# A two-layer hybrid decoder step on one Trainium2 core: gate and up products of the feed-forward by seven half products, gated rows kept in DRAM between two phases

## The chip, the core and the metric

One core of one Trainium2 (trn2) chip runs the whole step as one program. The metric is the device time in microseconds; the kernel before was timed in three runs. Everything is fp32 in and out.

## What is computed

Two layers (state-space heads with latent attention, then sliding-window attention), each followed by a gated feed-forward with a causal depthwise convolution on its gate branch. 1024 prompt tokens and 8 sample tokens share all weights; `D_MODEL` is 1024 and `D_FF` is 2816. The part that the change touches, per layer:

```python
h = rmsnorm(x, norm_ffn[layer])
def conv_ffn(h, buf, w_gate, w_up, conv_w, conv_b, w_down):
    t = h.shape[1]
    g = h @ w_gate
    u = h @ w_up
    gp = jnp.concatenate([buf.astype(g.dtype), g], axis=1)
    c = conv_b
    for j in range(CONV_W):
        c = c + conv_w[j] * gp[:, j:j + t]
    out = (jax.nn.gelu(c) * u) @ w_down
    return out, gp[:, -(CONV_W - 1):]
x = x + f
```

## The kernel before

Activations are held transposed: a feature tile of 128 partitions by all 1032 tokens (`NT`). There are 8 model tiles (`KD`) and 22 ff tiles (`KF`). Every fp32 operand of a product is split into a hi part (rounded to the format fp32r) and a lo part (what is left), and a product is three matmuls per tile and 344 columns (`TT`): weight hi by x hi (L137), weight lo by x hi (L138), weight hi by x lo (L139), in `Slabs.products`. The weights come through two slots ("slabs", `s` 0 and 1): SP loads one (`load`), GpSimd (the `pool` queue) writes its hi and lo (`split`, L121 and L123), TensorE multiplies it with all 1032 columns into the PSUM tile of the slot, and an engine reads that tile out and frees it.

The feed-forward goes in four groups of ff tiles (6, 6, 5, 5). For each ff tile: gate into slot 0, up into slot 1 (8 x 3 x 3 matmuls each). VectorE multiplies gate by `rstd` (the norm's scale per token, L1515), does the convolution from `g` to `c` (two small copies L1517 and L1518 for the state, a `tensor_scalar` L1519, and for either further tap an op of 8 and one of 1024 columns, L1520 to L1526), multiplies up by `rstd` (L1530), takes ACT's gelu times `u` (L1533), and after ACT's hi copy writes the lo part (L1536). All of a group's gated rows stay in SBUF; after the group, TensorE does its down products for the 8 model tiles, and VectorE adds each to x (L1547, L1551).

Ahead of it, the out-projection runs 3 passes (layer 0) or 2 (layer 1) of 8 products; in the last pass VectorE adds each tile to x (L1609) and then, by `norm_dve`, writes the lo part (L220) and adds the squares that ACT has made (L226). `norm_act` is ACT's part of this (hi, L212, and square, L215). The sum over the features is three matmuls (`norm_sums`), the root ACT's (`norm_roots`, L237), and the inverse three reciprocals of 344 columns on VectorE (`norm_inverse`, L244), which lie beside the first gate product. The first product waits tile by tile for the lo parts (`paced`).

Each engine has its own queue in program order; they wait for each other with semaphores, and nothing reorders them. `ch.link` is a wait of VectorE for its own earlier op.

## Time and profile before

| | |
|---|---|
| median of 3 runs | 3202.59 us (3201.11 to 3202.88) |
| span of the profiled execution | 3200.6 us |
| TensorE busy | 2998.8 us (94%), 23117 matmuls |
| VectorE busy | 1803.8 us (56%) |
| GpSimd busy | 872.4 us (27%) |
| ACT busy | 602.1 us (19%) |
| DRAM read, written | 189.87 MB, 6.25 MB |

The page gives one execution; its span runs from the first to the last instruction. "Busy" is a sum over instructions, so it says what an engine did and not what it was waited for. In rows of instructions "PE" is TensorE's matmul, "PEld" its weight load, "DVE" VectorE, "POOL" GpSimd. The order of an engine's queue is not in the profile; it is shown with the change.

### The profile page before, as it was taken

What the parts mean: (1) busy time and instruction counts of PE and PEld (TensorE: products, weight loads), DVE (VectorE), ACT (ScalarE), POOL (GpSimd) and SP (SyncE); (2) the same over time, 40 slices, a digit from 0 to 9 for tenths busy, and PEclk for the clock granted to TensorE, in tenths of its full rate; (3) what the DMA queues carried; (4) which work ended last, traced back from release to release, by engine and by line L of the source; (5) the groups of instructions that cost most, each with busy time, mean ns of one, the idle gap of its engine ahead of it and who ended that gap; (6) DMA issues with size and microseconds to landing.
All of it is one profiled execution on the core that took longest, in us unless ns stands there. A gap on an engine that the chain in (4) does not pass through costs nothing. (4 is left out here: it accounts for less than half of the span.)

```text
span 3200.6 us, 58571 instructions
## 1 busy us (share of the span) xinstructions
PE 2998.8 (94%) x23117; PEld 2623.7 (82%) x23117; DVE 1803.8 (56%) x2750; ACT 602.1 (19%) x1200; POOL 872.4 (27%) x496
## 2 busy tenths in 40 slices
PE   6967999998999899999999999998889999999997
PEld 6944666665555499999999999994589999999997
DVE  8895655565888645533515345667737515335254
ACT  3111544552000112100000001106512100000001
POOL 3200000100000045444344344420044344444442
PEclk8978999998999999999999999999989999999999
DMA  2100000004777521111111111202111111111112
GB/s 101 54 14 31 15 14 14 0 26 138 225 226 227 150 95 57 46 41 51 48 51 44 42 53 39 67 23 88 53 47 56 48 51 46 41 51 36 56 39 76
DMA packets 129157, 206.34 MB, mean 64 GB/s; under 512 B 14833, under 2 KB 95729, under 8 KB 128274
## 3 DMA queue, kind: packets, MB, share of 16 engines
q1 hardware_dynamic: 90994, 162.31, 16.2%
q10 hardware_dynamic: 38016, 41.99, 4.4%
q8 instruction: 102, 1.67, 0.2%
q14 instruction: 45, 0.37, 0.0%
HBM read 189.87 MB, written 6.25 MB: 61 GB/s over the span
## 5 line engine op out<-in xcount | busy, mean ns | idle before, releaser
L121 POOL TENSOR_TENSOR sb_slab_hi<-sb_slab_raw,sb_ones 128x1024 fp32r<-128x1024 f32 (+3 forms) x214 | 344.4, 1609 | 1719.0 <-PE ps_trunk_out L139 1053.1
L137 PE MATMUL ps_trunk_out<-sb_h_hi,sb_slab_hi 128*128 128x344 f32 x2400 | 768.0, 320 | 0.0
L138 PE MATMUL ps_trunk_out<-sb_h_hi,sb_slab_lo 128*128 128x344 f32 x2400 | 764.8, 319 | 0.0
L139 PE MATMUL ps_trunk_out<-sb_h_lo,sb_slab_hi 128*128 128x344 f32 x2400 | 764.4, 319 | 0.0
L123 POOL TENSOR_TENSOR sb_slab_lo<-sb_slab_raw,sb_slab_hi 128x1024 fp32r<-128x1024 f32 (+3 forms) x214 | 488.7, 2284 | 16.7
L138 PEld LDWEIGHTS ps_trunk_out<-sb_h_hi,sb_slab_lo 128*128 128x128 f32 x2400 | 450.4, 188 | 0.6
L137 PEld LDWEIGHTS ps_trunk_out<-sb_h_hi,sb_slab_hi 128*128 128x128 f32 x2400 | 450.3, 188 | 0.6
L139 PEld LDWEIGHTS ps_trunk_out<-sb_h_lo,sb_slab_hi 128*128 128x128 f32 x2400 | 450.4, 188 | 0.0
L137 PE MATMUL ps_trunk_out<-sb_ffn_a_hi,sb_slab_hi 128*128 128x344 f32 x1026 | 327.3, 319 | 5.0 <-DVEq L1538 5.0
L139 PE MATMUL ps_trunk_out<-sb_ffn_a_lo,sb_slab_hi 128*128 128x344 f32 x1026 | 328.3, 320 | 0.0
L138 PE MATMUL ps_trunk_out<-sb_ffn_a_hi,sb_slab_lo 128*128 128x344 f32 x1026 | 326.6, 318 | 0.0
L1246 PE MATMUL ps_dec_bank<-sb_dec_ckT,sb_dec_qc 32*32 32x256 f32 x4608 | 258.1, 377 | 8.2 <-DVE sb_dec_qc L1347 7.9
L1246 PEld LDWEIGHTS ps_dec_bank<-sb_dec_ckT,sb_dec_qc 32*32 32x32 f32 x4608 | 142.0, 106 | 118.9 <-issue 13.4
L1491 ACT ACTIVATE sb_ffn_a<-sb_ffn_c 128x1032 f32<-128x1032 f32 x44 | 47.0, 1068 | 997.3 <-DVEq L1528 997.3
L1547 DVE TENSOR_TENSOR sb_z<-sb_z,ps_trunk_out 128x1032 f32 x48 | 59.0, 1230 | 300.6 <-PE ps_trunk_out L139 300.6
L137 PEld LDWEIGHTS ps_trunk_out<-sb_ffn_a_hi,sb_slab_hi 128*128 128x128 f32 x1026 | 192.8, 188 | 6.1 <-DVEq L1538 6.1
L139 PEld LDWEIGHTS ps_trunk_out<-sb_ffn_a_lo,sb_slab_hi 128*128 128x128 f32 x1026 | 192.8, 188 | 0.0
L138 PEld LDWEIGHTS ps_trunk_out<-sb_ffn_a_hi,sb_slab_lo 128*128 128x128 f32 x1026 | 192.8, 188 | 0.0
L937 POOL TENSOR_TENSOR sb_mla_diag<-sb_ident,sb_mla_rinv 128x256 f32<-128x256 f32 x64 | 39.2, 613 | 558.9 <-DVE sb_mla_rinv L1117 558.9
L1330 DVE STREAM_TRANSPOSE sb_dec_ckT<-sb_dec_ck 128x1152 f32<-128x1152 f32 x128 | 172.8, 1361 | 26.5 <-DMA sb_dec_ck<-cache 25.7
L1515 DVE TENSOR_TENSOR sb_ffn_g<-ps_trunk_out,sb_rstd 128x1032 f32<-128x1032 f32 x44 | 54.2, 1233 | 232.3 <-PE ps_trunk_out L139 232.3
L988 PE MATMUL ps_mla_bank<-sb_mla_k,sb_mla_q 96*128 96x512 f32 (+3 forms) x384 | 150.1, 502 | 1.8 <-ACT sb_mla_v L1048 1.8
(412 smaller groups left out, 4559.6 us busy)
## 6 DMA issues: line engine op xcount, KB each, us to landing
sb_slab_raw<-f_w_gu SPq DMA_DIRECT2D x88, 512.0 KB, 3.5
sb_dec_ck<-cache SPq DMA_DIRECT2D x256, 144.0 KB, 3.1
sb_dec_ck<-cache ACTq DMA_DIRECT2D x256, 144.0 KB, 2.8
sb_slab_raw<-f_w_down SPq DMA_DIRECT2D x32, 384.0 KB, 3.1
sb_slab_raw<-f_w_down SPq DMA_DIRECT2D x32, 320.0 KB, 2.8
sb_slab_raw<-e_w_out SPq DMA_DIRECT2D x24, 256.0 KB, 2.6
sb_slab_raw<-o_w_in SPq DMA_DIRECT2D x12, 512.0 KB, 3.5
sb_slab_raw<-e_w_in SPq DMA_DIRECT2D x10, 512.0 KB, 3.5
```

The source lines that it names most:

```text
L121: nc.gpsimd.tensor_tensor(hi, raw, one, ALU.mult).then_inc(self.hi_done[s], 1)
L123: nc.gpsimd.tensor_tensor(self.lo[:, s, 0:kc, :], raw, hi.bitcast(F32), ALU.subtract).then_inc(self.split_done[s], 1)
L137: nc.tensor.matmul(out[:, t, 0:TT], a, x_hi(k)[:, cols], start=k == 0, stop=False)
L138: nc.tensor.matmul(out[:, t, 0:TT], b, x_hi(k)[:, cols], start=False, stop=False)
L139: last = nc.tensor.matmul(out[:, t, 0:TT], a, x_lo(k)[:, cols], start=False, stop=k == kc - 1)
L937: nc.gpsimd.tensor_tensor(diag[:, big], ident[:, :].unsqueeze(1).broadcast_to((P, 2, P)), rinv[:, 2 * big:2 * big + 2].unsqueeze(2).broadc ...
L988: m = MM(score(u)[:, c0:c1], qg[:, h, qb * P:(qb + 1) * P], kg[:, h, c0:c1], start=True, stop=True)
L1246: m = MM(bank[quads[b], x, half * 256:half * 256 + 256], qc[quads[b], (w // NU) % 2, j, :], ckT[quads[b], x, pages, 32 * j:32 * j + 32], s ...
L1330: m = V.transpose(ckT[:, w % 2, g * GP:(g + 1) * GP, :].rearrange("p a c -> p (a c)"), ck[:, w % CKS, g * GP:(g + 1) * GP, :].rearrange("p ...
L1491: nc.scalar.activation(a[:, :], c[:, :], ACT.Gelu_apprx_tanh).then_inc(ffn_act_done, 1)
L1515: ch.link(V.tensor_tensor(v3(g[:, 2:]), slabs.out[:, 0, :, 0:TT], v3(rstd), ALU.mult))
L1547: V.tensor_tensor(xm, xm, slabs.out[:, s, :, 0:TT], ALU.add).then_inc(slabs.free[s], 1)
```

## The change

Of a ff tile, gate and up together are a product of two blocks of weights by two halves of the 8 model tiles. With the tokens cut in two halves of 516 (`HT`), this is a 2x2 by 2x2 block product, and it is done by Strassen's scheme in Winograd's form: seven products q0 to q6 of half the depth (4 model tiles) and half the tokens, in place of eight. The names in it:

- **Inputs** (`X_OF`): the blocks B11, B21, B22 of x and the sums T1 to T4, made once per layer when the out-projection ends (`x_act` with the hi parts, `x_dve` and `x_dve_last` with the sums and lo parts, `ffn_enter_act` and `ffn_enter_dve` around them). The norm's `norm_dve` now only adds squares.
- **Weights**: VectorE makes four sums per pair of gate and up (`w_sum`, 128x512 each), ACT seven hi parts (`w_high`), GpSimd seven lo parts (128x512, L1620), in place of GpSimd's two hi and two lo of 128x1024.
- **Products**: each q is 4 tiles x 2 x 3 matmuls of 258 columns (`QT`), so 168 per pair in place of 144 of 344 columns. They go into four PSUM bank pairs: bA takes q0, q3 and q5, bC q1 and q6, bB q2, bD q4.
- **Combining**: ACT copies q0 out (`s1`); VectorE makes g and u by seven more ops of 516 columns. The first conv tap moves from VectorE to ACT.
- **`ffn_left`** counts what VectorE has taken out of the banks, 7 per pair. q0 of the next pair waits for 6, q1 for 7 (which is L1832, behind the convolution).
- **Gated rows**: `c` times `u`, not scaled for the up branch, goes to DRAM by SP (`keep`). In the second phase, groups of (4, 6, 6, 6), ACT's queue loads a group back (`a_load`), VectorE scales it by `rstd` (`a_scale`, L1727), ACT writes the hi part, VectorE the lo part (`a_low`, L1732), and TensorE does the down products as before, with waits for each tile's lo part in the first product of a group.
- **First pair**: TensorE does the norm's sums behind q4; the three reciprocals stand on VectorE between the second and third of its ops. SBUF places of other tensors move with it (`m_parts` takes the out-projection's parts in the other order).

Sums, split and loads:

```diff
+def w_sum(dve, at_pair, q):
+    n = at_pair.n
+    if q == 0:
+        dve.wait_ge(slabs.raw_in[1], n(16, 16 * W_BEFORE[at_pair.layer] + 16))
+        V.tensor_tensor(wt[:, :, :], w_up[0], w_up[1], ALU.add).then_inc(ffn_sum, 1)
+    elif q == 1:
+        dve.wait_ge(slabs.raw_in[0], n(16, 16 * W_BEFORE[at_pair.layer] + 16))
+        dve.wait_ge(ffn_sum, n(4, 1))
+        V.tensor_tensor(wt2[:, :, :], wt[:, :, :], w_gate[0], ALU.subtract).then_inc(ffn_sum, 1)
+    elif q == 2:
+        dve.wait_ge(ffn_lo, n(7, 2))
+        dve.wait_ge(ffn_sum, n(4, 2))
+        V.tensor_tensor(wt[:, :, :], wt2[:, :, :], w_gate[1], ALU.subtract).then_inc(ffn_sum, 1)
+    else:
+        V.tensor_tensor(w_up[0], w_gate[0], w_up[0], ALU.subtract).then_inc(ffn_sum, 1)
...
+    def keep(p):
+        sp.wait_ge(ffn_a, p.n(1, 1))
+        sp.dma_start(a_dram[layer, one(p.f())].rearrange("a p t -> p (a t)"), c[:, :]).then_inc(ffn_out, 16)
...
+    with sp.Fori(0, KF - 1) as ci:
+        p = Pair(layer, 0, ci)
+        for s in range(2):
+            sp.wait_ge(ffn_lo, p.n(7, 6 + s))
+            sp.dma_start(slabs.raw[:, s, :, :], rows(ci + 1, s)).then_inc(slabs.raw_in[s], 16)
+        keep(p)
+    for s in range(2):
+        sp.wait_ge(ffn_lo, Pair(layer, KF - 1).n(7, 6 + s))
+        slabs.load(sp, s, n, GROUPS[0], A["f_w_down"][layer, s, :, 0:GROUPS[0], :])
+    keep(Pair(layer, KF - 1))
...
+def ffn_pool(pool, layer, n):
+    slabs.rows += KF
+    with pool.Fori(0, KF) as ci:
+        p = Pair(layer, 0, ci)
+        for q in range(7):
+            pool.wait_ge(ffn_hi, p.n(7, q + 1))
+            nc.gpsimd.tensor_tensor(w_slot(slabs.lo, q), W_FROM[q], w_slot(slabs.hi, q).bitcast(F32),
+                                    ALU.subtract).then_inc(ffn_lo, 1)
+    end = Pair(layer, KF - 1)
+    pool.wait_ge(ffn_mm, end.n(7, 5))
+    slabs.split(pool, 0, n, GROUPS[0])
+    pool.wait_ge(ffn_mm, end.n(7, 7))
+    slabs.split(pool, 1, n, GROUPS[0])
```

Entry, VectorE's part:

```diff
+        low(T1, m, T1f(m), 2 * m + 2, g_m)
+        return
+    k = m - HK
+    f0, h0 = HK + 3 * k, 2 * HK + 6 * k + 1
+    t2, t3, t4 = T2f(k), T3f(k), T4f(k)
+    dve.wait_ge(x_hi_done, n_h + h0)
+    V.scalar_tensor_tensor(out=t3, in0=second, scalar=g_m, in1=t3, op0=ALU.mult, op1=ALU.subtract).then_inc(x_f32, 1)
+    low(B21, k, first, h0 + 1, g_m)
+    dve.wait_ge(x_f32, f_at(f0 + 1))
+    V.scalar_tensor_tensor(out=t2, in0=x[:, k, HALF[0]], scalar=gain(k), in1=t3, op0=ALU.mult, op1=ALU.add).then_inc(x_f32, 1)
+    dve.wait_ge(x_f32, f_at(f0 + 2))
+    V.scalar_tensor_tensor(out=t4, in0=first, scalar=g_m, in1=t2, op0=ALU.mult, op1=ALU.subtract).then_inc(x_f32, 1)
+    low(T2, k, t2, h0 + 2)
+    low(B22, k, second, h0 + 3, g_m)
+    low(T3, k, t3, h0 + 4)
```

TensorE:

```diff
+def ffn_pe(pe, layer, n, i, last_pair=None):
+    bA, bB, bC, bD = ffn_banks()
+    bank_of = (bA, bC, bB, bA, bD, bA, bC)
+    def product(p, q, paced=False):
+        pe.wait_ge(ffn_lo, p.n(7, q + 1))
+        whi, wlo = w_slot(slabs.hi, q), w_slot(slabs.lo, q)
+        for k in range(HK):
+            if paced:
+                pe.wait_ge(x_lo_done, x_lo_count(layer, q, k))
+            for h in range(2):
+                cols = slice(h * QT, (h + 1) * QT)
+                out, xh, xl = bank_of[q][:, h], X_OF[q](k, 0)[:, cols], X_OF[q](k, 1)[:, cols]
+                nc.tensor.matmul(out, whi[:, k, :], xh, start=k == 0, stop=False)
+                nc.tensor.matmul(out, wlo[:, k, :], xh, start=False, stop=False)
+                m = nc.tensor.matmul(out, whi[:, k, :], xl, start=False, stop=k == HK - 1)
+        m.then_inc(ffn_mm, 1)
+    def products(p, first=False):
+        for q in range(7):
+            if first and q in (0, 2):
+                pe.wait_ge(slabs.free[q // 2], n + 1)
+            if q == 0 and not first:
+                pe.wait_ge(ffn_left, p.n(7, -1))
+            if q == 1 and not first:
+                pe.wait_ge(ffn_left, p.n(7, 0))
+            if q == 3:
+                pe.wait_ge(ffn_copied, p.n(1, 1))
+            if q in (5, 6):
+                pe.wait_ge(ffn_left, p.n(7, q - 4))
+                if first:
+                    pe.wait_ge(norm_root, 3 * i + q - 4)
+            product(p, q, first)
+            if first and q == 4:
+                pe.wait_ge(ffn_left, p.n(7, 2))
+                ffn_sums(pe, i)
+    products(Pair(layer, 0), True)
+    with pe.Fori(0, KF - 1) as ci:
+        products(Pair(layer, 1, ci))
+    end = Pair(layer, KF - 1)
+    pe.wait_ge(ffn_left, end.n(7, 6))
     k0 = layer * KF
     for grp, gs in enumerate(GROUPS):
-        skip = 0
-        if grp == 0:
-            slabs.products(pe, 0, n, KD, hi, lo, gate_hooks)
-            slabs.products(pe, 1, n, KD, hi, lo, up_hooks)
-            skip = 1
-        with pe.Fori(0, gs - skip) as ci:
+        g_hi, g_lo = g_parts[grp]
+        mul_hi, mul_lo = lambda k: g_hi[:, k, :], lambda k: g_lo[:, k, :]
+        by_thirds = last_pair is not None and grp + 1 == len(GROUPS)
+        slabs.products(pe, 0, n, gs, mul_hi, mul_lo,
+                       {k: (lambda k=k: pe.wait_ge(ffn_alo, k0 + FIRST[grp] + k + 1)) for k in range(gs)})
+        slabs.products(pe, 1, n, gs, mul_hi, mul_lo)
+        with pe.Fori(0, KD // 2 - 1 - by_thirds) as mi:
...
-            last_pair(pe, n + gs + KD // 2 - 1, gs)
-        n += gs + KD // 2
```

Phase 2's pieces, ACT's pair and VectorE's pair:

```diff
+def a_scale(dve, layer, grp, k):
+    uses = (4, 4, 4, 4, 3, 3)[k]
+    dve.wait_ge(chunk_in[k], 32 + 16 * (layer * uses + grp + (1 if k < 4 else 0)))
+    part = g_f32[grp][:, k, :]
+    V.tensor_tensor(part, part, rstd[:, :], ALU.mult).then_inc(ffn_scaled, 1)
...
+        act.wait_ge(ffn_mm, p.n(7, 1))
+        nc.scalar.copy(two(s1), bA).then_inc(ffn_copied, 1)
+        w_high(act, p, 4)
+        w_high(act, p, 5)
+        if last:
+            a_load(act, layer, 0, range(GROUPS[0]))
+        w_high(act, p, 6)
+        if kind == "first":
+            ffn_roots(act, i)
+        if not last:
+            w_high(act, nxt, 0)
+        act.wait_ge(ffn_left, p.n(7, 4))
+        if kind != "first" or layer:
+            act.wait_ge(ffn_out, p.n(16, 0))
+        nc.scalar.activation(c[:, :], g[:, 2:], ACT.Identity, scale=tap(2), bias=tap(3)).then_inc(ffn_tapped, 1)
+        if last:
+            a_high(act, layer, 0, (0, 1))
+        else:
+            for q in (1, 2, 3):
+                w_high(act, nxt, q)
+        act.wait_ge(ffn_conv, p.n(1, 1))
+        nc.scalar.activation(c[:, :], c[:, :], ACT.Gelu_apprx_tanh).then_inc(ffn_tapped, 1)
...
+        dve.wait_ge(ffn_mm, p.n(7, 3))
+        dve.wait_ge(ffn_copied, p.n(1, 1))
+        ch.mark(V.tensor_tensor(bB, bB, two(s1), ALU.add))
+        dve.wait_ge(ffn_mm, p.n(7, 4))
+        ch.settle()
+        V.tensor_tensor(two(s1), bA, two(s1), ALU.add).then_inc(ffn_left, 1)
+        dve.wait_ge(ffn_left, p.n(7, 1))
+        V.tensor_tensor(two(u_half[1]), two(s1), bC, ALU.subtract).then_inc(ffn_left, 1)
+        if kind == "first":
+            norm_inverse(dve, ch, i)
+        V.tensor_tensor(two(g_half[0]), bB, two(r_half[0]), ALU.mult).then_inc(ffn_left, 1)
+        if end:
+            a_scale(dve, layer, 0, 0)
+            a_scale(dve, layer, 0, 1)
+        dve.wait_ge(ffn_mm, p.n(7, 5))
+        dve.wait_ge(ffn_left, p.n(7, 2))
+        ch.link(V.tensor_tensor(bD, two(u_half[1]), bD, ALU.subtract))
+        V.tensor_tensor(two(g_half[1]), bD, two(r_half[1]), ALU.mult).then_inc(ffn_left, 1)
+        if not end:
+            w_sum(dve, nxt, 0)
+            w_sum(dve, nxt, 1)
+        dve.wait_ge(ffn_mm, p.n(7, 6))
+        V.tensor_tensor(two(u_half[1]), bA, two(u_half[1]), ALU.add).then_inc(ffn_left, 1)
+        V.tensor_tensor(two(u_half[0]), bA, two(s1), ALU.add).then_inc(ffn_left, 1)
+        if end:
+            a_low(dve, layer, 0, 0)
+            a_low(dve, layer, 0, 1)
+        dve.wait_ge(ffn_left, p.n(7, 4))
+        V.tensor_copy(tail[:, one(f), :], g[:, T:T + 2])
+        V.tensor_copy(new[:, one(f), 1, :], g[:, 2 + T:2 + NT])
+        dve.wait_ge(ffn_tapped, p.n(2, 1))
+        ch.mark(V.scalar_tensor_tensor(out=c[:, T:NT], in0=old(1), scalar=tap(1), in1=c[:, T:NT],
+                                       op0=ALU.mult, op1=ALU.add))
+        ch.link(V.scalar_tensor_tensor(out=c[:, 0:T], in0=g[:, 1:1 + T], scalar=tap(1), in1=c[:, 0:T],
+                                       op0=ALU.mult, op1=ALU.add))
+        ch.mark(V.scalar_tensor_tensor(out=c[:, T:NT], in0=old(0), scalar=tap(0), in1=c[:, T:NT],
+                                       op0=ALU.mult, op1=ALU.add))
+        V.scalar_tensor_tensor(out=c[:, 0:T], in0=g[:, 0:T], scalar=tap(0), in1=c[:, 0:T],
+                               op0=ALU.mult, op1=ALU.add).then_inc(ffn_conv, 1)
+        dve.wait_ge(ffn_mm, p.n(7, 7))
+        dve.wait_ge(ffn_left, p.n(7, 6))
+        V.tensor_tensor(two(u_half[0]), bC, two(u_half[0]), ALU.add).then_inc(ffn_left, 1)
+        if end:
+            for k in (2, 3):
+                a_scale(dve, layer, 0, k)
+            for k in (2, 3):
+                a_low(dve, layer, 0, k)
+        else:
+            w_sum(dve, nxt, 2)
+            w_sum(dve, nxt, 3)
+        dve.wait_ge(ffn_tapped, p.n(2, 2))
+        dve.wait_ge(ffn_left, p.n(7, 7))
+        V.tensor_tensor(c[:, :], c[:, :], u[:, :], ALU.mult).then_inc(ffn_a, 1)
```

How the order moves. VectorE's queue for one ff tile in the loop of the kernel before (register and semaphore rows left out):

```order
L1515 TENSOR_TENSOR sb_ffn_g<-ps_trunk_out,sb_rstd 128x1032 [waits slab_mm_done0]
L1517 COPY sb_ffn_tail<-sb_ffn_g 128x2
L1518 COPY sb_ffn_new<-sb_ffn_g 128x8
L1519 TENSOR_SCALAR sb_ffn_c<-sb_ffn_g,sb_ffn_taps 128x1032
L1520 SCALAR_TENSOR_TENSOR sb_ffn_c<-sb_ffn_past,sb_ffn_taps,sb_ffn_c 128x8
L1522 SCALAR_TENSOR_TENSOR sb_ffn_c<-sb_ffn_g,sb_ffn_taps,sb_ffn_c 128x1024
L1524 SCALAR_TENSOR_TENSOR sb_ffn_c<-sb_ffn_past,sb_ffn_taps,sb_ffn_c 128x8
L1526 SCALAR_TENSOR_TENSOR sb_ffn_c<-sb_ffn_g,sb_ffn_taps,sb_ffn_c 128x1024 [waits dve_chain]
L1530 TENSOR_TENSOR sb_ffn_u<-sb_rstd,ps_trunk_out 128x1032 [waits dve_chain,slab_mm_done1]
L1533 TENSOR_TENSOR sb_ffn_a<-sb_ffn_a,sb_ffn_u 128x1032 [waits ffn_gelu]
L1536 TENSOR_TENSOR sb_ffn_a_lo<-sb_ffn_a,sb_ffn_a_hi 128x1032
```

And for one pair of the changed kernel, from the op behind g1 on (`sb_ffn_wt` and `sb_ffn_wt_12508` are the two sums of weights, `ps_trunk_extra` the bank pair bC):

```order
L1552 TENSOR_TENSOR sb_ffn_wt<-sb_slab_raw 128x512 [waits slab_raw_in1]
L1556 TENSOR_TENSOR sb_ffn_wt_12508<-sb_ffn_wt,sb_slab_raw 128x512 [waits ffn_sum_done]
L1813 TENSOR_TENSOR sb_ffn_u<-ps_trunk_out,sb_ffn_u 128x516 [waits ffn_product_done]
L1814 TENSOR_TENSOR sb_ffn_u<-ps_trunk_out,sb_ffn_s_12509 128x516
L1819 COPY sb_ffn_tail<-sb_ffn_g 128x2
L1820 COPY sb_ffn_new<-sb_ffn_g 128x8
L1822 SCALAR_TENSOR_TENSOR sb_ffn_c<-sb_ffn_past,sb_ffn_taps,sb_ffn_c 128x8
L1824 SCALAR_TENSOR_TENSOR sb_ffn_c<-sb_ffn_g,sb_ffn_taps,sb_ffn_c 128x1024
L1826 SCALAR_TENSOR_TENSOR sb_ffn_c<-sb_ffn_past,sb_ffn_taps,sb_ffn_c 128x8
L1828 SCALAR_TENSOR_TENSOR sb_ffn_c<-sb_ffn_g,sb_ffn_taps,sb_ffn_c 128x1024
L1832 TENSOR_TENSOR sb_ffn_u<-ps_trunk_extra,sb_ffn_u 128x516 [waits ffn_bank_left,ffn_product_done]
L1560 TENSOR_TENSOR sb_ffn_wt<-sb_ffn_wt_12508,sb_slab_raw 128x512 [waits ffn_sum_done]
```

L1832 releases bC; ahead of it now stand two weight sums, two combining ops and the four conv ops, where before L1530, behind the conv, freed the tile of up, which the next up product needs only after the next gate product.

VectorE's queue at the end of the last pair, ahead of the first down product (`sb_ffn_a_f_12522` is the group's gated rows as loaded back, `sb_ffn_a_1_12515` its lo part; "x2" is two tiles):

```order
L1828 SCALAR_TENSOR_TENSOR sb_ffn_c<-sb_ffn_g,sb_ffn_taps,sb_ffn_c 128x1024
L1832 TENSOR_TENSOR sb_ffn_u<-ps_trunk_extra,sb_ffn_u 128x516 [waits ffn_bank_left,ffn_product_done]
L1727 TENSOR_TENSOR sb_ffn_a_f_12522<-sb_ffn_a_f_12522,sb_rstd 128x1032 [waits chunk_in2]
L1732 TENSOR_TENSOR sb_ffn_a_1_12515<-sb_ffn_a_f_12522,sb_ffn_a_0_12514 128x1032 [waits ffn_a_hi] x2
L1843 TENSOR_TENSOR sb_ffn_c<-sb_ffn_c,sb_ffn_u 128x1032 [waits ffn_bank_left,ffn_tap_and_gelu]
L1858 TENSOR_TENSOR sb_z<-sb_z,ps_trunk_out 128x1032 [waits slab_mm_done0]
```

The scaling and the lo parts of tiles 2 and 3, for which the first down product waits, stand behind the last conv op and L1832, and L1843, for which SP's last store waits, behind them.

## Rows read from the trace of the kernel before

**Rows 1.** The page: span and busy time by engine.
```profile
span 3200.6 us, 58571 instructions
...
PE 2998.8 (94%) x23117; PEld 2623.7 (82%) x23117; DVE 1803.8 (56%) x2750; ACT 602.1 (19%) x1200; POOL 872.4 (27%) x496
```

**Rows 2.** The page's costliest groups: matmul L137, its weight load.
```profile
L137 PE MATMUL ps_trunk_out<-sb_h_hi,sb_slab_hi 128*128 128x344 f32 x2400 | 768.0, 320 | 0.0
...
L137 PEld LDWEIGHTS ps_trunk_out<-sb_h_hi,sb_slab_hi 128*128 128x128 f32 x2400 | 450.3, 188 | 0.6
```

**Rows 3.** Windows of the first feed-forward (columns: window, us, engines' busy, PEclk, DMA, GB/s).
```profile
1400.00:1700.00 300.00, 300.00 (x1915) 300.00 (x1915) 107.21 (x95) 15.95 (x15) 124.42 (x62) 1.00 0.15 47
...
sum 750.80, PE 747.26 PEld 745.85 DVE 341.79 ACT 75.36 POOL 311.90; mean PE 149.45 PEld 149.17 DVE 68.36 ACT 15.07 POOL 62.38
```

**Rows 4.** A window of the second feed-forward, same columns.
```profile
2500.00:3160.00 660.00, 657.56 (x4194) 656.99 (x4193) 273.69 (x243) 50.61 (x47) 270.03 (x135) 1.00 0.15 46
```

**Rows 5.** Timeline (start, duration, engine, line), TensorE and VectorE, product boundary.
```profile
1706.50 0.31 PE L139 MATMUL ps_trunk_out<-sb_h_lo,sb_slab_hi 128*128 128x344 f32 x1
...
1706.65 0.32 PE L137 MATMUL ps_trunk_out<-sb_h_hi,sb_slab_hi 128*128 128x344 f32 x1
...
1706.85 1.23 DVE L1515 TENSOR_TENSOR sb_ffn_g<-ps_trunk_out,sb_rstd 128x1032 f32<-128x1032 f32 x1 [4.83 <-PE ps_trunk_out L139]
```

**Rows 6.** Window of the 128-column products L654.
```profile
177.30:184.80 7.50, 7.40 (x64) 7.21 (x64) 1.00 0.00 0
```

**Rows 7.** VectorE lines, ns min/median/max: conv L1526, PSUM copy L1929.
```profile
L1526 DVE SCALAR_TENSOR_TENSOR sb_ffn_c<-sb_ffn_g,sb_ffn_taps,sb_ffn_c x44: 1284/1285/1285, 1288.8 to 3114.1; 128x1024 f32<-128x1024 f32 x44
...
L1929 DVE COPY sb_swa_probT<-ps_swa_bank x32: 683/691/693, 2180.0 to 2306.4; 128x512 f32<-128x512 f32 x32
```

**Rows 8.** Timeline of VectorE, small ops of the first ff tile.
```profile
1285.60 0.17 DVE L1517 COPY sb_ffn_tail<-sb_ffn_g 128x2 f32 x1 [0.24 <-DVE sb_ffn_g L1515]
...
1285.74 0.17 DVE L1518 COPY sb_ffn_new<-sb_ffn_g 128x8 f32 x1
...
1287.01 0.23 DVE L1520 SCALAR_TENSOR_TENSOR sb_ffn_c<-sb_ffn_past,sb_ffn_taps,sb_ffn_c 128x8 f32<-128x8 f32 x1 [0.17 <-DVE sb_ffn_c L1519]
```

**Rows 9.** Timeline of VectorE, last out-projection pass.
```profile
1235.38 1.23 DVE L1609 TENSOR_TENSOR sb_z<-sb_z,ps_trunk_out 128x1032 f32<-128x1032 f32 x1 [3.23 <-PE ps_trunk_out L139]
...
1236.52 2.40 DVE L220 SCALAR_TENSOR_TENSOR sb_h_lo<-sb_z,sb_gains,sb_h_hi 128x1032 fp32r<-128x1032 f32 x1
...
1241.04 1.23 DVE L1609 TENSOR_TENSOR sb_z<-sb_z,ps_trunk_out 128x1032 f32<-128x1032 f32 x1 [0.97 <-PE ps_trunk_out L139]
...
1242.19 1.29 DVE L220 SCALAR_TENSOR_TENSOR sb_h_lo<-sb_z,sb_gains,sb_h_hi 128x1032 fp32r<-128x1032 f32 x1
```

**Rows 10.** Timeline of GpSimd, the same stretch.
```profile
1235.42 1.04 POOL L121 TENSOR_TENSOR sb_slab_hi<-sb_slab_raw,sb_ones 128x512 fp32r<-128x512 f32 x1 [2.13 <-PE ps_trunk_out L139]
...
1236.54 1.29 POOL L123 TENSOR_TENSOR sb_slab_lo<-sb_slab_raw,sb_slab_hi 128x512 fp32r<-128x512 f32 x1
...
1242.27 2.36 POOL L123 TENSOR_TENSOR sb_slab_lo<-sb_slab_raw,sb_slab_hi 128x512 fp32r<-128x512 f32 x1
```

**Rows 11.** ACT's gelu, ns min/median/max.
```profile
L1491 ACT ACTIVATE sb_ffn_a<-sb_ffn_c x44: 1065/1067/1077, 1290.2 to 3115.5; 128x1032 f32<-128x1032 f32 x44
```

**Rows 12.** Window with loads of x and weights (columns as rows 3).
```profile
1120.00:1125.00 5.00, 0.37 (x1) 0.38 (x2) 5.00 (x4) 4.65 (x5) 3.94 (x3) 0.50 1.01 402
```

**Rows 13.** The reciprocals L244, ns min/median/max.
```profile
L244 DVE RECIPROCAL sb_rstd<-sb_rstd x12: 2244/2303/2304, 38.8 to 2444.5; 128x344 f32<-128x344 f32 x12
```

**Rows 14.** TensorE after idleness: timeline, and window (columns as rows 3).
```profile
22.34 0.66 PE L137 MATMUL ps_w_in_out<-sb_h_hi,sb_slab_hi 128*128 128x344 f32 x1 [2.81 <-DVE sb_h_lo L220]
...
22.30:28.30 6.00, 5.96 (x21) 5.96 (x22) 6.00 (x6) 4.33 (x5) 0.00 (x0) 0.50 0.21 81
```

**Rows 15.** VectorE's lo part L1536, ns min/median/max.
```profile
L1536 DVE TENSOR_TENSOR sb_ffn_a_lo<-sb_ffn_a,sb_ffn_a_hi x44: 1232/1975/1982, 1294.4 to 3125.1; 128x1032 f32 x44
```

**Rows 16.** The page's loads of 256 KB: count, size, median us to landing.
```profile
sb_slab_raw<-e_w_out SPq DMA_DIRECT2D x24, 256.0 KB, 2.6
```

More of the change, by code:

```diff
@@ L103, in __init__ @@
         self.used = 0
+        self.rows = 0
     def take(self, pairs):
@@ new lines, in build, with one, __init__, f @@
+        W_SLOT = (1, 3, 2, 0, 1, 3, 2)
+        w_slot = lambda t, q: t[:, W_SLOT[q] // 2, HK * (W_SLOT[q] % 2):HK * (W_SLOT[q] % 2) + HK, :]
+        X_OF = (B11, T1, B21, T2, B22, T3, T4)
+        two = lambda ap: ap.rearrange("p (a b) -> p a b", a=2)
+        W_BEFORE = {}
+        XF, XH, XL = 16, 32, 28
+        def one(f):
+            return slice(f, f + 1) if isinstance(f, int) else bass.ds(f, 1)
+        class Pair:
+            def __init__(self, layer, f0, ci=0):
+                self.layer, self.f0, self.j0, self.ci = layer, f0, layer * KF + f0, ci
+            def f(self, d=0):
+                return self.ci + (self.f0 + d)
+            def n(self, per, more):
+                return self.ci * per + (self.j0 * per + more)
@@ new lines, in ffn_banks, with ffn_sum_at, ffn_sums @@
+        def ffn_banks():
+            flat = slabs.out.rearrange("p a b c -> p (a b) c")
+            return flat[:, 0:2, 0:QT], flat[:, 4:6, 0:QT], extra[:, 0:2, 0:QT], flat[:, 2:4, 0:QT]
+        ST = TT // 2
+        def ffn_sum_at(t):
+            flat = slabs.out.rearrange("p a b c -> p (a b) c")
+            return (flat[:, 0:2], extra, flat[:, 4:6])[t][:, :, QT:QT + ST]
+        def ffn_sums(pe, i):
+            pe.wait_ge(norm_added, 7 * i + 7)
+            for t in range(3):
+                for h in range(2):
+                    c0 = t * TT + h * ST
+                    m = nc.tensor.matmul(ffn_sum_at(t)[:, h], ones[:, :], acc[:, c0:c0 + ST], start=True, stop=True)
+                m.then_inc(norm_sum, 1)
@@ new lines, in ffn_dve, with pair @@
+        def ffn_dve(dve, ch, layer, n, i, x, last, count=KD):
+            bA, bB, bC, bD = ffn_banks()
+            CH = 5
+            def pair(p, kind):
+                nxt = Pair(layer, p.f0 + 1, p.ci)
+                end = kind == "last"
+                f = p.f()
+                tap = lambda q: taps[:, one(f), q:q + 1].rearrange("p a b -> p (a b)")
+                old = lambda q: past[:, one(f), q, :].rearrange("p a b -> p (a b)")
+                dve.wait_ge(ffn_mm, p.n(7, 3))
[45 more added lines that the diff above has]
+                        a_low(dve, layer, 0, k)
+                else:
+                    w_sum(dve, nxt, 2)
[3 more added lines that the diff above has]
+                V.tensor_tensor(c[:, :], c[:, :], u[:, :], ALU.mult).then_inc(ffn_a, 1)
@@ new lines, in ffn_dve @@
+            pair(Pair(layer, 0), "first")
+            with dve.Fori(0, KF - 2) as ci:
+                ch.enter(ci, CH)
+                pair(Pair(layer, 1, ci), "")
+            ch.leave(KF - 2, CH)
+            pair(Pair(layer, KF - 1), "last")
+            for grp, gs in enumerate(GROUPS):
+                final = grp + 1 == len(GROUPS)
+                for m in range(count if final else KD):
+                    dve.wait_ge(slabs.mm_done[m % 2], n + m // 2 + 2)
+                    V.tensor_tensor(v3(x[:, m, :]), v3(x[:, m, :]), slabs.out[:, m % 2, :, 0:TT],
+                                    ALU.add).then_inc(slabs.free[m % 2], 1)
+                    if final:
+                        last(m)
+                    else:
+                        if m < GROUPS[grp + 1]:
+                            a_scale(dve, layer, grp + 1, m)
+                        if 1 <= m <= GROUPS[grp + 1]:
+                            a_low(dve, layer, grp + 1, m - 1)
+                n += KD // 2
```

369 lines of the change are left out of this document (222 added, 147 removed).

## Prediction

> **What bounds the kernel now.** I read the page first, then the matmul groups, the windows of the first feed-forward, and its timeline. The page has TensorE busy for 2998.8 of 3200.6 us and VectorE for 56% [rows 1]. Most of it is 344-column matmuls in groups of 2400, three per weight tile [rows 2]. In the first feed-forward (1263.5 to 2014.3, 750.8 us) TensorE is busy for 747.26 us, at granted clock 1.00 [rows 3]; the second looks alike, 657.56 busy in 660 [rows 4]. There are 1915 matmuls in the 300 us of 1400 to 1700, one every 0.157 us [rows 3], as the starts at 1706.50 and 1706.65 also show [rows 5], so a ff tile's gate and up, 144 matmuls, take 22.56 us, and the down products, 1584 per layer, 248.2. TensorE's column stream alone bounds this part. VectorE and GpSimd have slack, since they see a product only every 11.3 us.
>
> The profiled execution spans 3200.6 us; the runs' median is 3202.59. I add differences to the median. A difference of 0.2% is 6.4 us, about what a measurement of this kernel can tell from none.
>
> **The matmuls.** A ff tile now takes 7 x 24 = 168 matmuls of 258 columns. That is 43344 columns instead of 49536. Nothing in the trace has this shape. Scaling 0.157 us by columns gives 117.5 ns. The nearest rows on the fast side are 64 weight loads with 128 columns in 7.21 us, 113 ns apart [rows 6]; on the slow side, a start every 157 ns however narrow [rows 3]. A weight load lasts 188 ns and overlaps the matmul before it [rows 2]; at 113 ns it still kept up, so width and not the load should set the pace. I take 118 ns: a product 2.83 us, a pair 19.8 (bounds 19.0 and 26.3). Alone this gains 2.74 us per pair, 60 per layer, 120 in all. The rest is what the waits give back.
>
> Behind this stands the Trainium skill, "TensorE: Matmul & The Clock Gate", section "Back-to-back issue gap": columns over 2.4 GHz plus 2.5 ns. It would give 110 ns here, but 146 ns for 344 columns, where the rows show 157; so the rule is 7% short and the measured pitch stands. By it the period below would be 20.65.
>
> **The steady pair.** There are four PSUM bank pairs for seven products. Product q1 of the next pair overwrites the bank of q6, so it waits for L1832, the last VectorE op on that bank (ffn_left 7). L1832 is queued behind the conv. Count from the end of q5: TensorE has q6 and the next q0 to run, 5.66 us. VectorE must do, in its order of the change: hop from TensorE 0.20 (the product boundary at 1706.65 and L1515 at 1706.85 [rows 5]), but it is in the second weight sum until about 0.8; L1813 and L1814, 516 columns from PSUM, 0.62 start to start each (512 columns 0.69 whole [rows 7], 1032 columns 1.23 [rows 5]); the bank-left wait and two small copies 0.5 (0.17 each at 1285.60 and 1285.74, with a wait of 0.24 before [rows 8]); a small conv op, 0.15; L1824, 1.20; a small one with its wait, 0.26; L1828, 1.20; L1832, 0.69 (conv ops of 1024 columns last 1.28, of 8 columns 0.23, and the next starts 0.08 before an op's end where it needn't wait [rows 7 to 9]). Sum 6.0, and 0.1 from L1832 to TensorE: 6.1.
>
> **The port.** Two-input SBUF ops on VectorE and GpSimd's reads exclude each other whole: at 1242.19 VectorE's L220 takes 1.29 and GpSimd's L123, started 0.08 later, 2.36; at 1236.54 it is the other way round, L123 1.29 and L220 2.40 [rows 9, 10]. With a PSUM input there is no wait (L1609 at 1235.38, 1.23, beside L121 at 1235.42, 1.04). Before, POOL did four ops a ff tile; now it does seven 512-column subtractions of 1.29 = 9.0 us in 21, and their hi halves come from ACT in the same stretch as the conv. VectorE has now four weight sums, two conv ops, the product with u: 8.1 us of such ops. The third subtraction for the next pair falls just ahead of the second small conv op and the first delays weight sum 0. I price this at 1.1 us on the chain, one GpSimd op less what is hidden (bounds 0 and 2.6, two ops).
>
> This agrees with the Trainium skill, "SBUF — State Buffer", section "Who interferes with whom": a VectorE instruction with two SBUF inputs contends with a GpSimd read, and whoever comes first holds the port for its whole instruction. It speaks against a change that adds such ops on both engines; without it the chain would be 6.1 and the period 20.25.
>
> So the chain is 7.2, and the period 7.2 + 5 products (14.15) = 21.35; I use **21.4** against 22.56. TensorE sits 1.55 us at q1 in each pair. For 20 pairs per layer: 428 against 451.2.
>
> ACT has eight 512-column copies and two of 1032 columns per pair, the latter 1.07 each and the former about half of it plus a little, 0.59: 6.8 us [rows 11], not a bound. The added store of a is 0.5 MB per ff tile, 25 GB/s in 21 us, beside 45 to 47 before [rows 3, 4], while the chip moved 402 in 1120 to 1125 [rows 12]: hidden in phase 1.
>
> **Entry.** In the last out-projection pass a product comes every 5.66 us (L1609 at 1235.38 and 1241.04), and VectorE had for each the add 1.23, L220 1.29 to 2.40 and L226 [rows 9]. Now a chunk m >= 4 has the add (1.15 to the next start), seven 516-column ops (about 0.66 each: four low halves, three sums; half a 1032-column op of 1.23 to 1.29), L226's add 1.22, own-chain waits of 0.5 and some 0.7 of port waits: 8.2 us, 2.5 behind per product. The chain from the end of the fourth-last product is 3 x 8.25 + 2 (port, last weight ops) + 1.07 (ACT's square) + 0.59 (hi half) + 1.29 (POOL's low half) = 29.7, against 3 x 5.66 = 17.0 of TensorE work: the first product starts **13 us** late. Bounds: 5 (no port waits, sums hidden) and 18.
>
> **First pair.** 19.8 of work; q4 waits about 2 for its weights; the norm sums 0.9; then the reciprocals, 3 x 2.3 = 6.9 [rows 13], now sit on VectorE between q5's and q2's use and hold all banks: about 6 exposed (before they lay beside products). After 2.81 us of idleness TensorE was granted 0.50, the 1.2 GHz level, for the next 6.00 us: 21 matmuls of 344 columns, one every 0.286 us [rows 14]: 3 more. Together **32**. The second pair inherits VectorE's lag: **23.5**.
>
> **Phase 2.** The same 1584 matmuls, 248.2. At its start the first product needs a of tiles 0 to 3 scaled and split: L1727 and L1732 for k = 2, 3 are queued on VectorE behind conv and L1832, four ops of 1.23 to 1.98 [rows 15]: TensorE waits about 7.4 us at k = 2. The third product waits about 3.9 for its weights: SP has the last store of a, which waits for L1843, ahead of that load. L1843 2.3, issue 0.3, the store and behind it the load 3.4 + 2.6, the split 1.04 + 1.29 [rows 10, 16] make 10.9 from the last L1732, against 1.4 + 5.66 of products. With the lower clock after both, some 12 us at double pitch (6 lost), and 1.5 at group boundaries: **267** (bounds 250 and 285). Leaving the loop costs 1.
>
> **Sum per layer**: 13 + 32 + 23.5 + 428 + 1 + 267 = 764.5 against 750.9, so +13.6; two layers +27. 3202.6 + 27 = **3230 us**.
>
> **Rivals.**
> - *The conv does not meet GpSimd.* POOL's subtractions slide into VectorE's waits for TensorE, the chain shrinks towards 6.1, the pair to 20.0. For it: ops settle into a repeated pattern, and L1526 was 1.28 in all 44 before [rows 7]. Against it: POOL is busy 9 of 21 us, and L1536 does get stretched, median 1975 against 1232 ns [rows 15]. Entry 11, first 31, second 21.5, 400, 1, 264: 728.5, so -22.4 per layer, 3158 us: **faster**. The change pays from a mean period of 20.7 downwards ((764.5 - 750.9) / 20 = 0.7 below 21.4).
> - *The matmul is faster than by columns*, 113 ns [rows 6]. The chain stays 7.2, and 7.2 + 5 x 2.71 = 20.75; 0.6 x 40 = 25 back: 3205 us, the same.
> - *The pitch does not shrink with the width* [rows 3]: 26.3 per pair; the chain (7.2 < 7.5) is then hidden. 11 + 36 + 26.5 + 526 + 1 + 267 = 867.5, +233: 3436 us.
> - *VectorE meets GpSimd twice per pair* in the chain: 8.7, period 22.85, +1.45 x 40: 3288 us.
>
> **Chances.** Forecast 0.48; port conflict missed 0.27; matmul faster, same, 0.13; two conflicts 0.08; pitch fixed 0.04. The forecast's own spread by the entry's and phase 2's bounds, (-8, +5) and (-17, +18) per layer, is -50 to +46 at the ends, which are hardly all met: mostly +0 to +50. Part of the forecast case thus lands within 6.4 us or lower, and part of the third lands faster. Faster 0.30, same 0.12, slower 0.58. The range leaves out the fixed pitch and the extremes: 3160 to 3280.
>
> **What would show it.** In the changed profile: L1671 starts 0.118 apart; pairs 21.4 apart in the loop with an idle gap of about 1.5 us before the first L1671 on ps_trunk_extra (q1), released by L1832; L1824 or L1828 or the small ones stretched past 1.28 and 0.23, POOL L1620 above 1.29; L1671's first start 13 us after the last out product; a TensorE gap of 6 us in the first pair released by VectorE (L1801 behind L244); 7 us at the first product of phase 2 waiting for L1732; PEclk 0.50 after these. It would be wrong if the gap at q1 is under 0.5 us or above 3, if the pitch isn't near 118 ns, or if phase 2's 248 us of matmuls are starved by the loads of a.

## The result, and the profile after

The changed kernel takes 3324.14 us (median of 4 runs, 3323.15 to 3327.47) against 3201.98 (median of 4) for the kernel before: ratio 1.0382, 95% interval 1.037 to 1.0394. It is slower, as forecast, but by 122 us and not 27, and above the range of 3160 to 3280. The profiled execution spans 3321.4 us, 120.8 more than the one before.

The page, with the span, the busy times and the granted clock by slice, which answer to [rows 1]:

```profile
span 3321.4 us, 62894 instructions
...
PE 2968.4 (89%) x24185; PEld 2584.0 (78%) x24185; DVE 2138.1 (64%) x3306; ACT 863.3 (26%) x1634; POOL 913.1 (27%) x628
...
PEclk9989999998999898999999999999898999998999
```

TensorE is busy 30 us less than before, in a span 121 us longer: matmul work was removed, and idle time came. VectorE has gone from 1803.8 to 2138.1 us. The page's clock digits hide what happens: the slices of the feed-forward read 8 or 9, and nearly all slices of the kernel before did too.

What TensorE waited for (the view of waits, TensorE's rows; total us, times, longest):

```profile
PE ps_trunk_extra L1671 <- DVE sb_ffn_u L1832: 90.8, 42, 2.2
...
PE ps_trunk_out L138 <- POOL sb_slab_lo L124: 28.1, 4, 9.5
...
PE ps_trunk_out L1671 <- issue: 23.4, 2, 11.7
...
PE ps_trunk_out L138 <- DVE sb_ffn_a L1732: 15.6, 6, 6.4
...
PE ps_trunk_out L1671 <- DVE sb_ffn_u L1814: 10.3, 2, 5.1
```

The first row is the wait at q1 that the forecast named, for L1832, 42 times and 2.16 us each on average. The others are the entry ("issue", 11.7 us per layer), the third down product's weights (5.65 us per layer; the rest of that row lies ahead of the feed-forward), the lo parts of the gated rows, and the first pair.

To see where the time went, the first layer is cut at the same places as in the forecast, by the starts in TensorE's timeline:

```profile
1275.88 0.55 PE L1671 MATMUL ps_trunk_out<-sb_ffn_x,sb_slab_hi 128*128 128x258 f32 x1 [11.69 <-issue]
...
1307.03 0.58 PE L1671 MATMUL ps_trunk_out<-sb_ffn_x,sb_slab_hi 128*128 128x258 f32 x1 [5.15 <-DVE sb_ffn_u L1814]
...
1809.09 0.40 PE L138 MATMUL ps_trunk_out<-sb_ffn_a,sb_slab_hi 128*128 128x344 f32 x1 [0.75 <-DVE sb_ffn_a L1732]
...
1835.46 0.65 PE L138 MATMUL ps_trunk_out<-sb_ffn_a,sb_slab_hi 128*128 128x344 f32 x1 [5.65 <-POOL sb_slab_lo L124]
...
2075.02 0.32 PE L140 MATMUL ps_trunk_out<-sb_ffn_a,sb_slab_hi 128*128 128x344 f32 x1
```

| stretch of layer 0 | forecast | measured |
|---|---|---|
| first product late (1263.51 before, 1275.88 now) | 13 | 12.4 |
| first pair, to q0 of the second | 32 | 31.2 |
| second to last pair, to the first down product | 451.5 | 502.1 |
| phase 2, and leaving the loop | 268 | 266.2 |
| sum | 764.5 | 811.8 (750.8 before) |

(The parts are rounded singly.) Everything but the loop came within 2 us. The loop cost 50.6 us more per layer than forecast, and 2 x 50.6 is the 95 us between 27 and 122, to within what the other terms are off.

**One pair of the loop.** TensorE's stall, and VectorE and GpSimd beside it (start, duration, engine, line; in brackets the idle time before):

```profile
1520.24 0.60 DVE L1819 COPY sb_ffn_tail<-sb_ffn_g 128x2 f32 x1
...
1520.97 1.27 DVE L1824 SCALAR_TENSOR_TENSOR sb_ffn_c<-sb_ffn_g,sb_ffn_taps,sb_ffn_c 128x1024 f32<-128x1024 f32 x1
...
1522.40 1.20 DVE L1826 SCALAR_TENSOR_TENSOR sb_ffn_c<-sb_ffn_past,sb_ffn_taps,sb_ffn_c 128x8 f32<-128x8 f32 x1 [0.16 <-DVE sb_ffn_c L1824]
...
1523.52 2.37 DVE L1828 SCALAR_TENSOR_TENSOR sb_ffn_c<-sb_ffn_g,sb_ffn_taps,sb_ffn_c 128x1024 f32<-128x1024 f32 x1
...
1525.82 0.68 DVE L1832 TENSOR_TENSOR sb_ffn_u<-ps_trunk_extra,sb_ffn_u 128x516 f32<-128x516 f32 x1
...
1521.59 0.62 ACT L1576 CAST sb_slab_hi<-sb_slab_raw 128x512 fp32r<-128x512 f32 x1 [2.14 <-PE ps_trunk_extra L1673]
1522.12 0.61 ACT L1576 CAST sb_slab_hi<-sb_ffn_wt 128x512 fp32r<-128x512 f32 x1
...
1519.53 1.29 POOL L1620 TENSOR_TENSOR sb_slab_lo<-sb_ffn_wt,sb_slab_hi 128x512 fp32r<-128x512 f32 x1 [1.68 <-ACT sb_slab_hi L1576]
1522.29 1.29 POOL L1620 TENSOR_TENSOR sb_slab_lo<-sb_slab_raw,sb_slab_hi 128x512 fp32r<-128x512 f32 x1 [1.47 <-ACT sb_slab_hi L1576]
...
1523.54 1.28 POOL L1620 TENSOR_TENSOR sb_slab_lo<-sb_ffn_wt,sb_slab_hi 128x512 fp32r<-128x512 f32 x1
...
1526.63 0.58 PE L1671 MATMUL ps_trunk_extra<-sb_ffn_x,sb_slab_hi 128*128 128x258 f32 x1 [2.21 <-DVE sb_ffn_u L1832]
```

L1826, an op of 8 columns, took 1.20 us instead of the 0.23 of [rows 8], because GpSimd's subtraction had started 0.11 earlier; then GpSimd's next one, started 0.02 after L1828, ran at its own 1.28 us while L1828 took 2.37 instead of 1.28. VectorE met GpSimd twice there, and not once. A smaller meeting lies ahead of these two: the copy L1819, 2 columns, took 0.60 us instead of the 0.17 of [rows 8], and ended with the GpSimd op that had started at 1519.53. So it is in nearly every pair (VectorE's lines, ns min/median/max):

```profile
L1819 DVE COPY sb_ffn_tail<-sb_ffn_g x44: 157/618/1248, 1306.8 to 3034.5; 128x2 f32 x40, 128x2 f32<-128x2 f32 x4
...
L1826 DVE SCALAR_TENSOR_TENSOR sb_ffn_c<-sb_ffn_past,sb_ffn_taps,sb_ffn_c x44: 226/1195/1212, 1311.0 to 3036.1; 128x8 f32<-128x8 f32 x44
...
L1828 DVE SCALAR_TENSOR_TENSOR sb_ffn_c<-sb_ffn_g,sb_ffn_taps,sb_ffn_c x44: 1277/2370/2373, 1311.2 to 3036.2; 128x1024 f32<-128x1024 f32 x44
```

Here the trace agrees with the Trainium skill, "SBUF — State Buffer", section "Who interferes with whom", that one holds the port for its whole instruction and the other waits: GpSimd's ops run at their own 1.28 us, and VectorE's are longer by 0.97 and 1.09 us. At L1826 it was GpSimd that had come first, by 0.11 us; at L1828 the order can't be read off, since it and GpSimd's second op start within 0.02 us.

**The clock.** Windows of the same pair (columns as [rows 3]):

```profile
1525.00:1527.00 2.00, 0.37 (x1) 0.38 (x2) 2.00 (x3) 1.07 (x2) 0.00 (x0) 0.86 0.00 0
...
1527.00:1529.00 2.00, 2.00 (x11) 2.00 (x11) 1.84 (x3) 0.99 (x2) 0.94 (x1) 0.50 0.00 0
...
1529.00:1531.00 2.00, 2.00 (x15) 2.00 (x15) 0.00 (x0) 0.00 (x0) 0.98 (x1) 0.78 0.59 241
...
1531.00:1533.00 2.00, 2.00 (x19) 2.00 (x18) 0.00 (x0) 0.62 (x1) 1.06 (x1) 1.00 0.06 23
```

After the stall the granted clock is 0.50, the 1.2 GHz level, for about three microseconds: the window shows 11 matmuls in two microseconds instead of 19. Starts of L1832 are 23.9 to 24.1 us apart in 17 of the 20 periods between the first pair and the last. In three periods of each layer they are 22.5 apart, with no fall of the clock: in the first of them the stall was 1.1 us, in the other two the same 2.2. So the clock fell after 18 of the 20 stalls of 2.2 us in each layer (the 18th lies at the last pair). The stall at 1335.8 is one that was spared:

```profile
1334.00:1336.00 2.00, 0.29 (x2) 0.30 (x3) 2.00 (x3) 0.99 (x2) 0.00 (x0) 1.00 0.00 0
...
1336.00:1338.00 2.00, 2.00 (x19) 2.00 (x19) 1.93 (x3) 1.07 (x3) 0.85 (x1) 1.00 0.00 0
```

So a pair is 20.0 us of matmuls (0.119 us apart, forecast 0.118), 2.5 of stall with its hops, and 1.5 of clock. Against the forecast's 21.4 that is 1.1 us in each of 20 periods and 1.5 more in 17 of them, about 48 of the 50.6 us.

### The profile page after: what moved, and what is told of

It reads as the page before. It is cut to its first block and busy times, and to the rows that moved or that the text cites. A ratio compares the mean times of both kernels' runs of the same rounds, so it can differ in the third digit from the quotient of the medians.

```text
span 3321.4 us, 62894 instructions
## 1 busy us (share of the span) xinstructions
PE 2968.4 (89%) x24185; PEld 2584.0 (78%) x24185; DVE 2138.1 (64%) x3306; ACT 863.3 (26%) x1634; POOL 913.1 (27%) x628
## 5 line engine op out<-in xcount | busy, mean ns | idle before, releaser
L1671 PE MATMUL ps_trunk_out<-sb_ffn_x,sb_slab_hi 128*128 128x258 f32 x1760 | 501.7, 285 | 36.7 <-issue 23.4
L1673 PE MATMUL ps_trunk_out<-sb_ffn_x,sb_slab_hi 128*128 128x258 f32 x1760 | 499.7, 284 | 0.0
L1672 PE MATMUL ps_trunk_out<-sb_ffn_x,sb_slab_lo 128*128 128x258 f32 x1760 | 499.4, 284 | 0.0
L1671 PEld LDWEIGHTS ps_trunk_out<-sb_ffn_x,sb_slab_hi 128*128 128x128 f32 x1760 | 336.2, 191 | 38.0 <-issue 34.6
L138 PE MATMUL ps_trunk_out<-sb_ffn_a,sb_slab_hi 128*128 128x344 f32 x1020 | 329.9, 323 | 27.0 <-DVE sb_ffn_a L1732 15.6
L1620 POOL TENSOR_TENSOR sb_slab_lo<-sb_slab_raw,sb_slab_hi 128x512 fp32r<-128x512 f32 x176 | 227.0, 1290 | 421.6 <-ACT sb_slab_hi L1576 421.6
L1672 PEld LDWEIGHTS ps_trunk_out<-sb_ffn_x,sb_slab_lo 128*128 128x128 f32 x1760 | 336.5, 191 | 0.0
L1673 PEld LDWEIGHTS ps_trunk_out<-sb_ffn_x,sb_slab_hi 128*128 128x128 f32 x1760 | 336.4, 191 | 0.0
L140 PE MATMUL ps_trunk_out<-sb_ffn_a,sb_slab_hi 128*128 128x344 f32 x1020 | 329.5, 323 | 0.0
L139 PE MATMUL ps_trunk_out<-sb_ffn_a,sb_slab_lo 128*128 128x344 f32 x1020 | 328.2, 322 | 0.0
L1671 PE MATMUL ps_trunk_extra<-sb_ffn_x,sb_slab_hi 128*128 128x258 f32 x704 | 228.7, 325 | 90.8 <-DVE sb_ffn_u L1832 90.8
L124 POOL TENSOR_TENSOR sb_slab_lo<-sb_slab_raw,sb_slab_hi 128x512 fp32r<-128x512 f32 (+2 forms) x126 | 271.8, 2157 | 9.9
L1620 POOL TENSOR_TENSOR sb_slab_lo<-sb_ffn_wt,sb_slab_hi 128x512 fp32r<-128x512 f32 x132 | 197.4, 1495 | 242.0 <-ACT sb_slab_hi L1576 242.0
L1672 PE MATMUL ps_trunk_extra<-sb_ffn_x,sb_slab_lo 128*128 128x258 f32 x704 | 223.6, 318 | 0.0
L1673 PE MATMUL ps_trunk_extra<-sb_ffn_x,sb_slab_hi 128*128 128x258 f32 x704 | 221.8, 315 | 0.0
```

What stands on the lines that cost most here:

```text
L124: nc.gpsimd.tensor_tensor(self.lo[:, s, 0:kc, :], raw, hi.bitcast(F32), ALU.subtract).then_inc(self.split_done[s], 1)
L138: nc.tensor.matmul(out[:, t, 0:TT], a, x_hi(k)[:, cols], start=k == 0, stop=False)
L139: nc.tensor.matmul(out[:, t, 0:TT], b, x_hi(k)[:, cols], start=False, stop=False)
L140: last = nc.tensor.matmul(out[:, t, 0:TT], a, x_lo(k)[:, cols], start=False, stop=k == kc - 1)
L1620: nc.gpsimd.tensor_tensor(w_slot(slabs.lo, q), W_FROM[q], w_slot(slabs.hi, q).bitcast(F32), ALU.subtract).then_inc(ffn_lo, 1)
L1671: nc.tensor.matmul(out, whi[:, k, :], xh, start=k == 0, stop=False)
```

## The experiments

All were timed in three rounds beside the kernel before, whose median in the three groups of runs was 3202.5, 3202.5 and 3202.1 us. The theory (A): the loop is bound by the release of bC behind the conv; the stall and the lower clock after it are the whole loss. Its rivals: the two engines are full anyway, so that the wait only moves (B); the clock falls for another reason than the stall (C).

**1. bC read ahead of the second tap** (`e1_bank_before_tap`). The three lines of L1832 move between the two large conv ops:

```diff
 ch.link(V.scalar_tensor_tensor(out=c[:, 0:T], in0=g[:, 1:1 + T], scalar=tap(1), in1=c[:, 0:T], ...))
+dve.wait_ge(ffn_mm, p.n(7, 7))
+dve.wait_ge(ffn_left, p.n(7, 6))
+V.tensor_tensor(two(u_half[0]), bC, two(u_half[0]), ALU.add).then_inc(ffn_left, 1)
 ch.mark(V.scalar_tensor_tensor(out=c[:, T:NT], in0=old(0), scalar=tap(0), in1=c[:, T:NT], ...))
 V.scalar_tensor_tensor(out=c[:, 0:T], in0=g[:, 0:T], scalar=tap(0), in1=c[:, 0:T], ...).then_inc(ffn_conv, 1)
-dve.wait_ge(ffn_mm, p.n(7, 7))
-dve.wait_ge(ffn_left, p.n(7, 6))
-V.tensor_tensor(two(u_half[0]), bC, two(u_half[0]), ALU.add).then_inc(ffn_left, 1)
```

> VectorE's read of bC (u0 += bC, which lets q1 of the next pair start) stands between the two large conv ops instead of behind both; nothing else is changed. Theory A (the loop is bound by the release of bC behind the conv, and the lower clock after each stall is its follow-up): VectorE reads bC about 3.6 us earlier, the stall of 2.21 us goes, the clock stays at 1.00, the pair falls from 24.05 to 20.0 to 20.3 us, so 42 pairs x 3.9 = 160 us less: 3150 to 3175 us, faster than the kernel before (3202). Rival B (VectorE and GpSimd together are full; the wait moves to the weights or to the copy of q0): pair 22 to 23.5 us, 3230 to 3300 us. Rival C (the lower clock does not come from the stall): pair 21.8, stall gone but about 1.5 us of half-speed matmuls per pair left, 3225 to 3240 us.

Measured: 3170.81 us, ratio to the kernel before 0.9904 (0.9887 to 0.992), 153 us less than the changed kernel. A pair is 20.08 us throughout. A window of its loop (columns as [rows 3]), and its second tap's ops on VectorE, here L1829 and L1831:

```profile
1400.00:1500.00 100.00, 100.00 (x839) 100.00 (x838) 73.92 (x100) 33.65 (x50) 45.14 (x35) 1.00 0.23 78
...
L1829 DVE SCALAR_TENSOR_TENSOR sb_ffn_c<-sb_ffn_past,sb_ffn_taps,sb_ffn_c x44: 216/560/565, 1310.6 to 2884.1; 128x8 f32<-128x8 f32 x44
...
L1831 DVE SCALAR_TENSOR_TENSOR sb_ffn_c<-sb_ffn_g,sb_ffn_taps,sb_ffn_c x44: 1277/2385/2392, 1310.8 to 2884.3; 128x1024 f32<-128x1024 f32 x44
```

TensorE is busy for the whole window at clock 1.00. The ops still meet GpSimd (560 and 2385 ns), but nothing that TensorE needs is behind them. B and C fall here: the period is TensorE's own, and 74% busy on VectorE leaves room. DRAM traffic isn't a cause either, since this loop carries it in full (78 GB/s) at TensorE's own pace.

**2. GpSimd's two subtractions behind the conv** (`e2_gpsimd_after_conv`):

```diff
-for q in (1, 2, 3):
-    w_high(act, nxt, q)
+w_high(act, nxt, 1)
 act.wait_ge(ffn_conv, p.n(1, 1))
 nc.scalar.activation(c[:, :], c[:, :], ACT.Gelu_apprx_tanh).then_inc(ffn_tapped, 1)
+if not last:
+    for q in (2, 3):
+        w_high(act, nxt, q)
```

> ACT makes the hi parts of the next pair's q2 and q3 behind the gelu instead of ahead of it, so that GpSimd's two subtractions no longer fall beside the conv. Theory A: L1826 goes back from 1.20 to 0.23 us and L1828 from 2.37 to 1.28, the chain that frees bC is 2.1 us shorter, the stall falls from 2.21 to 0.1 to 0.3 us and the clock stays up: pair 20.1 to 20.6 us, 3165 to 3190 us; if q2 then waits for its weights, up to 21.3, 3215 us. Rival B (not the port but something else stretches them): both stay near 1.2 and 2.4 us, pair about 24, 3320 us.

Measured: 3205.94 us, ratio 1.0013 (1.0004 to 1.0023). The same two ops, here L1828 and L1830, and VectorE's read of bC (here L1834), TensorE's starts at q1 and at q2, and GpSimd's op for q2 in one pair (timeline):

```profile
L1828 DVE SCALAR_TENSOR_TENSOR sb_ffn_c<-sb_ffn_past,sb_ffn_taps,sb_ffn_c x44: 225/227/228, 1307.7 to 2916.0; 128x8 f32<-128x8 f32 x44
...
L1830 DVE SCALAR_TENSOR_TENSOR sb_ffn_c<-sb_ffn_g,sb_ffn_taps,sb_ffn_c x44: 1276/1279/1280, 1307.8 to 2916.2; 128x1024 f32<-128x1024 f32 x44
...
1519.01 0.69 DVE L1834 TENSOR_TENSOR sb_ffn_u<-ps_trunk_extra,sb_ffn_u 128x516 f32<-128x516 f32 x1
...
1519.41 0.28 PE L1673 MATMUL ps_trunk_out<-sb_ffn_x,sb_slab_hi 128*128 128x258 f32 x1
1519.83 0.38 PE L1671 MATMUL ps_trunk_extra<-sb_ffn_x,sb_slab_hi 128*128 128x258 f32 x1
...
1520.78 2.41 POOL L1620 TENSOR_TENSOR sb_slab_lo<-sb_slab_raw,sb_slab_hi 128x512 fp32r<-128x512 f32 x1 [4.69 <-ACT sb_slab_hi L1576]
...
1523.24 0.39 PE L1671 MATMUL ps_trunk_out<-sb_ffn_x,sb_slab_hi 128*128 128x258 f32 x1 [0.25 <-POOL sb_slab_lo L1620]
```

Both ops are at their own durations in all 44 pairs, by an edit that touches neither: what ran beside them was the cause. The edit moves ACT's two ops with GpSimd's, but in the changed kernel ACT's were over at 1522.73, ahead of most of L1828's 2.37 us, so it was GpSimd's. The clock stays at 1.00. A pair is 21.0 us, not 20.1 to 20.6. Of the 0.9 us above the 20.08 of experiment 1, about 0.4 are still the release of bC, since q1 starts 0.42 us after the matmul ahead of it instead of 0.12, and about 0.5 are the late weights of q2 (1523.24). GpSimd's op for them takes 2.41 us, since it now lies beside two-input ops of VectorE (from 1520.21 to 1522.05). That the weights would be late is the case for which up to 3215 us was named; that the release would also still bind is what the expectation had as 0.1 to 0.3.

**3. The stall filled** (`e3_filler_in_stall`, then `e6_half_filler` with 9 and `e8_five_fillers` with 5):

```diff
 if q == 1 and not first:
+    pe.wait_ge(ffn_lo, p.n(7, 2))
+    w0, x0 = w_slot(slabs.hi, 1), X_OF[0](0, 0)
+    for r in range(18):
+        nc.tensor.matmul(bD_spare, w0[:, r % 4, :], x0[:, 0:254], start=True, stop=True)
     pe.wait_ge(ffn_left, p.n(7, 0))
```

`bD_spare` is 254 columns of a PSUM bank that no product uses.

> 18 matmuls of 254 columns into unused columns of a PSUM bank stand on TensorE ahead of the wait for bC: the chain on VectorE is unchanged, only TensorE is kept busy in the stall. Theory A (the stall itself costs 2.21 us, and another 1.5 us come from the lower clock after it): granted clock 1.00 throughout the loop, stall 0.1 to 0.3 us left, pair 22.5 us as in the three pairs that kept the clock, about 40 x 1.5 = 60 us less: 3260 to 3270 us. Rival C (the clock falls for another reason than the idle time): pair stays 24, 3320 us or more.

Measured: 3273.9 us, ratio 1.0222 (1.0205 to 1.0239). The pair is 22.50 us, and the clock stays up; a window of this kernel, and the same one of the changed kernel:

```profile
1400.00:1500.00 100.00, 99.81 (x827) 98.78 (x826) 68.57 (x87) 31.01 (x46) 44.28 (x32) 1.00 0.20 68
```

```profile
1400.00:1500.00 100.00, 91.12 (x706) 90.31 (x705) 65.17 (x87) 28.43 (x42) 40.78 (x31) 0.93 0.18 63
```

50 us come back with not one useful instruction more, which is the price of the clock: 2 x 17 pairs x 1.5. C falls. The time is 4 us above the 3260 to 3270 expected. The next two leave part of the stall idle; the forecast had a stall of 1.55 us.

> As the filler run, with 9 matmuls in place of 18, so that 1.1 to 1.2 us of the 2.21 us stall stay idle. The chain on VectorE stays as it is, so the pair is 22.5 us if the granted clock stays at 1.00 (3270 to 3278 us) and 24 us if it falls as without filler (3320 us). It tells whether a stall of the length that the forecast had (1.55 us) would also have cost clock: if the pair is 22.5, the clock loss is a consequence of the stall having been longer than forecast; if 24, the forecast left it out in any case.

> As the filler runs, with 5 matmuls, which leaves 1.6 us of the 2.21 us stall idle, the length that the forecast had. The pair is 22.5 us, 3270 to 3275 us, if the clock stays up at that length, as it did with 1.1 us idle; 24 us, 3320 us, if it falls as with 2.21 us. A mixture of pairs of both lengths is possible, since even at 2.21 us three pairs of each layer kept the clock.

Measured: 3271.83 us (ratio 1.0215, 1.0198 to 1.0232) with 9, and 3266.6 us (1.0207, 1.019 to 1.0224) with 5. All loop pairs are 22.5 us in both; the median of the second is 3 us below what was expected. The wait that is left, with its longest, of the run with 9 and of the run with 5:

```profile
PE ps_trunk_extra L1672 <- DVE sb_ffn_u L1837: 43.8, 40, 1.1
```

```profile
PE ps_trunk_extra L1672 <- DVE sb_ffn_u L1837: 63.4, 42, 1.6
...
1400.00:1500.00 100.00, 92.18 (x763) 91.18 (x762) 67.75 (x87) 30.60 (x45) 43.43 (x32) 1.00 0.20 69
```

With 1.1 and with 1.6 us idle in every pair the clock stayed at 1.00; with 2.2 it fell after 18 of 20 stalls in each layer. So, as far as pairs of 22.5 us can tell it for one of 21.4, a stall of the forecast length would not have cost clock, and the clock loss is a consequence of the port's second wait. Why two stalls of 2.2 us in each layer are spared stays open.

**4. The last store of a behind the next weight loads** (`e4_store_after_loads`):

```diff
+for s in range(2):
+    slabs.load(sp, s, n + 1, GROUPS[0], A["f_w_down"][layer, s + 2, :, 0:GROUPS[0], :])
 keep(Pair(layer, KF - 1))
 for grp, gs in enumerate(GROUPS):
-    skip = grp == 0
+    skip = 2 * (grp == 0)
```

> SP issues the weight loads of the third and fourth down product ahead of the last store of a, instead of behind it. Theory A: TensorE's wait of 5.65 us for GpSimd's L124 at the third down product goes, or falls below 1 us, in both layers, and some of the lower clock after it: 12 to 16 us less, 3308 to 3312 us. Rival (the loads are slow because the loads of a fill the queues, so starting them earlier changes little): under 4 us less, 3320 us or more.

Measured: 3311.0 us, ratio 1.034 (1.0323 to 1.0357), 13.1 us less. The wait for GpSimd's lo parts:

```profile
PE ps_trunk_out L138 <- POOL sb_slab_lo L124: 16.8, 2, 9.5
```

28.1 us in 4 times have become 16.8 in 2; the two that went are the 5.65 us of each layer, and the two that stay are ahead of the feed-forward.

**5. Together** (`e5_tap_and_store`: 1 and 4; `e7_split_before_conv`: besides, in the last pair tiles 2 and 3 are scaled and split ahead of the conv; the lines taken out behind it and ACT's part are not shown):

```diff
 if end:
     a_low(dve, layer, 0, 0)
     a_low(dve, layer, 0, 1)
+    for k in (2, 3):
+        a_scale(dve, layer, 0, k)
+    for k in (2, 3):
+        a_low(dve, layer, 0, k)
```

> Both edits together: the read of bC ahead of the second tap, and the last store of a behind the early weight loads. The two lie in different stretches, so theory A adds their gains: 3170.8 less 13 = 3158 us (3154 to 3162). Rival: the 5.65 us at the third down product turn into another wait when phase 1 ends sooner after its loads: 3165 to 3171 us.

> As the two edits together, and in the last pair the scaling and the lo parts of tiles 2 and 3 stand ahead of the convolution on VectorE (with ACT's hi parts ahead of its gelu). Theory A: TensorE's wait for L1732 at k = 2 of the first down product falls from 6.4 us to 2.5 to 3.5 in each layer, a little clock with it: 6 to 9 us less than the two edits, 3149 to 3153 us. Rival (VectorE merely passes the delay on to the adds of the first down products): under 2 us less, 3156 us or more.

Measured: 3154.31 us (ratio 0.9852, 0.9836 to 0.9869) and 3148.4 us (0.9836, 0.9819 to 0.9852). TensorE's wait for the lo parts, of the first and of the second:

```profile
PE ps_trunk_out L138 <- DVE sb_ffn_a L1734: 14.9, 6, 6.4
```

```profile
PE ps_trunk_out L138 <- DVE sb_ffn_a L1734: 7.8, 6, 2.9
```

The gains add: 153 and 13 make 3158, measured 3154. The third edit took 5.9 us, where 6 to 9 were expected. The last kernel is 54 us faster than the one before, out of the 120 us that the fewer columns are worth. What it still gives away per layer is the late first product (11.7 us idle) and the 5.1 us in the first pair behind the reciprocals; no other order was tried for these.

## Why the prediction was wrong

- **The matmuls**: 118 ns forecast, 0.119 us measured (a pair 20.0 us against 19.8). Right. The formula of the Trainium skill ("TensorE: Matmul & The Clock Gate", "Back-to-back issue gap"), which that section gives as the gap of an isolated matmul, makes 110 ns at 258 columns and 146 at 344. The trace doesn't agree: the formula is 8% short of the 119 ns here and 7% short of the 157 before. The period by it was also added up wrongly: 7.2 + 5 x 2.64 is 20.4 and not 20.65; nothing in the forecast hangs on it.
- **The chain and its place**: right. The stall is at q1, the releaser L1832, the only large wait in the loop; moving L1832 alone took it away. One step of the chain came out by luck: the 0.5 us for a semaphore wait and two small copies were 0.60, with no such wait and with GpSimd's op in its place (L1819).
- **The port**: this step failed, "I price this at 1.1 us on the chain, one GpSimd op less what is hidden (bounds 0 and 2.6, two ops)". It was 0.97 at L1826 and 1.09 at L1828, 2.1 in all. The 0.97 came with the first GpSimd op as reckoned; what was missed is that ACT makes the hi parts of q2 and q3 one behind the other, so that GpSimd's second subtraction is ready when the first ends, and L1828 waits for all of it. That ACT's two hi parts, and so GpSimd's two ops, follow each other stood in the changed code. The forecast's 8.1 us of two-input ops on VectorE per pair, from which no term was worked out, were 6.5 by the ops' own durations (four sums of 0.68, two of 1.28, one of 1.22). VectorE's backlog at the start of the chain was 0.5 and not 0.8. So the chain is 8.1 us (end of q5 at 1518.54, q1 at 1526.63) and not 7.2, and a pair without a clock loss 22.5; the fourth rival, with two meetings, had 22.85 and got a chance of 0.08, and its 3288 us lay outside the stated range of 3160 to 3280, though only the fixed pitch and the extremes were said to be left out.
- **The clock**: the second step that failed is a term left out of the sum. The forecast charged the 1.2 GHz level after the first pair's and phase 2's waits of 5 us and more and nothing after the one in the loop. That fits a stall of 1.55 us, as the runs with 1.1 and 1.6 us idle show, but the upper bound of the port's price had to carry it: with 2.2 us idle came 1.5 us more in 17 of 20 periods. By that, 22.5 became 24.05. The 2.6 bound would have given 22.85 + 1.5 = 24.35 and 3230 + 40 x 2.95 = 3348 us, and the range would have held the result.
- **Entry, first pair, phase 2**: 12.4, 31.2 and 266.2 us against 13, 32 and 268. Right in sum. By parts, two errors of phase 2 partly cancel: 6.44 us at k = 2 (forecast 7.4) and 5.65 at the third product's weights (3.9); in the first pair it was 5.15 behind the reciprocals (about 6).
- **The direction**: right, and for the reason given. The result lies beyond the slowest case but the fixed pitch, the one with two meetings.

## What to carry to other kernels

The fewer columns paid here only as far as the waits they brought stayed small. Give the queue of the engine that frees a PSUM bank the freeing op first, and the work that nothing waits for after it; one op moved was worth 153 us here. Where VectorE ops share a stretch with GpSimd ops, count every GpSimd op that is ready in that stretch, up to its whole duration (here 0.97 and 1.09 us of 1.28), and in either direction. A stall that returns in every iteration can cost TensorE's clock on top of itself (here 1.5 us behind 2.2), so the upper end of a range for such a stall needs the clock's term.

## What was not expected of the hardware

The clock's loss did not grow evenly with the stall: none in the runs with 1.1 and 1.6 us idle per pair, 1.5 us in most pairs of the one with 2.2. And an op of 8 columns can hold VectorE for 1.20 us, as it waits for GpSimd's whole op; a small op in such a stretch is priced by what runs beside it and not by its size.
